# Two-block network on one core: the local-attention chain of each head pair is spread over more of the next pair's projections

## What is computed

```python
def second_block(x, ...):
    for l in range(DEPTH):                      # 2 layers
        h = rms_norm_2(x, mix_norm_g[l])
        proj = h @ w_in[l]
        sb_q, sb_k, sb_v, sw_q, sw_k, sw_v, gate_logits = jnp.split(proj, split_at, axis=-1)
        o_sb = stick_breaking_attention(sb_q, sb_k, sb_v)
        q = apply_rope(rms_norm_2(sw_q, q_norm_g[l]), cos, sin)
        k = apply_rope(rms_norm_2(sw_k, k_norm_g[l]), cos, sin)
        y_swa = sliding_window_sink_attention(q, k, sw_v, sinks[l]) @ w_branch_swa[l]
        ...
        x = x + merged @ w_out[l]
        x = x + jnp.square(jax.nn.relu(rms_norm_2(x, mlp_norm_g[l]) @ w_up[l])) @ w_down[l]

def sliding_window_sink_attention(q, k, v, sinks):
    # a block of 128 queries sees its own block of keys and the one before it
    scores = jnp.einsum('bnqkgd,bnskd->bnkgqs', qb, k_band) * scale
    scores = jnp.where(valid, scores, -jnp.inf)
    probs = jax.nn.softmax(jnp.concatenate([scores, sink], axis=-1), axis=-1)[..., :-1]
    return jnp.einsum('bnkgqs,bnskd->bnqkgd', probs, v_band)
```

## Time and profile before

| | us |
|---|---|
| runs | 2957.77, 2960.5, 2960.77 |
| profiled execution | 2960.41 |
| its span, first to last instruction | 2958.6 |
| TensorE busy | 2815.6 (95%) |
| VectorE busy | 1515.0 (51%) |
| ScalarE busy | 1167.7 (39%) |
| GpSimd busy | 89.5 (3%) |

### The profile page before, as it was taken

One profiled execution on the slowest core, in us unless ns is written; L12 is line 12 of the kernel. 1 busy time (PEld: TensorE's weight loads), 2 busy tenths in 40 slices (PEclk: granted clock), 3 DMA queues, 4 the chain that ended last, 5 costly groups with the idle time before them and its releaser, 6 DMA issues.

```text
span 2958.6 us, 30829 instructions
## 1 busy us (share of the span) xinstructions
PE 2815.6 (95%) x12462; PEld 2219.0 (75%) x12462; DVE 1515.0 (51%) x2101; ACT 1167.7 (39%) x1736; POOL 89.5 (3%) x64
## 2 busy tenths in 40 slices
PE   7799889999998999998999999999989999999998
PEld 6677777888877888886555788888865657888887
DVE  3555557564767666577334445343543434544343
ACT  4443325343456433244444434222434444333222
POOL 1321210000000000000000000000000000000000
PEclk9899999999998999999999999999999999999999
DMA  3111112222322322222111122222221112222322
GB/s 142 54 54 54 43 41 78 100 94 99 106 87 79 112 100 93 100 96 89 36 36 43 57 93 100 99 94 100 94 71 36 41 38 71 93 96 97 100 96 75
DMA packets 66813, 235.66 MB, mean 80 GB/s; under 512 B 7408, under 2 KB 8176, under 8 KB 66672
## 3 DMA queue, kind: packets, MB, share of 16 engines
q1 hardware_dynamic: 62064, 226.00, 22.3%
q10 hardware_dynamic: 4608, 7.70, 0.7%
HBM read 231.57 MB, written 2.10 MB: 79 GB/s over the span
## 4 chain that ended last, share of the span: by engine, by line
PE 87%; DVE 7%; ACT 4%; issue 1%; POOL 0%; ACTq 0%; DVEq 0%
PE bank L392 25%; PE bank L394 25%; PE bank L393 25%; ACT w_hi_k L839 1%; PE bank L700 1%; PE bank L711 1%; PE bank L749 1%; DVE w_lo_k L1290 1%; PE bank L691 1%; PE bank L703 1%; PE bank L760 1%; PE bank L767 1%; DVE xr_lru L1577 1%; PE bank L527 0%; DVE land_r_mix L1413 0%
## 5 line engine op out<-in xcount | busy, mean ns | idle before, releaser
L392 PE MATMUL bank<-x_hi_k,w_hi_k 128*128 128x512 f32 x2152 | 883.2, 410 | 22.9 <-DVE x_lo_k L1297 18.5
L839 ACT ACTIVATE w_hi_k<-raw_k 128x1024 fp32r<-128x1024 f32 x431 | 454.6, 1058 | 1012.5 <-PE bank L394 1012.4
L394 PE MATMUL bank<-x_hi_k,w_lo_k 128*128 128x512 f32 x2152 | 849.6, 395 | 0.0
L393 PE MATMUL bank<-x_lo_k,w_hi_k 128*128 128x512 f32 x2152 | 848.4, 394 | 0.0
L1290 DVE TENSOR_TENSOR w_lo_k<-raw_k,w_hi_k 128x1024 fp32r<-128x1024 f32 x431 | 528.8, 1227 | 182.4 <-ACT w_hi_k L839 182.3
L392 PEld LDWEIGHTS bank<-x_hi_k,w_hi_k 128*128 128x128 f32 x2152 | 412.2, 192 | 115.2 <-DVE x_lo_k L1297 20.5
L393 PEld LDWEIGHTS bank<-x_lo_k,w_hi_k 128*128 128x128 f32 x2152 | 411.7, 191 | 86.9 <-issue 5.7
L394 PEld LDWEIGHTS bank<-x_hi_k,w_lo_k 128*128 128x128 f32 x2152 | 410.1, 191 | 88.7
L392 PE MATMUL bank<-y_hi_k,w_hi_k 128*128 128x512 f32 x1136 | 448.2, 395 | 15.5 <-DVE w_lo_k L1290 7.6
L394 PE MATMUL bank<-y_hi_k,w_lo_k 128*128 128x512 f32 x1136 | 444.6, 391 | 0.0
L393 PE MATMUL bank<-y_lo_k,w_hi_k 128*128 128x512 f32 x1136 | 444.4, 391 | 0.0
(11 more groups left out here) (319 smaller groups left out, 2562.1 us busy)
## 6 DMA issues: line engine op xcount, KB each, us to landing
raw_k<-wstream SPq DMA_DIRECT2D x431, 512.0 KB, 3.2
h_k<-xT ACTq DMA_DIRECT2D x8, 256.0 KB, 7.7
outT<-h_k ACTq DMA_DIRECT2D x8, 256.0 KB, 3.3
decay_mix<-constants ACTq DMA_DIRECT2D x4, 256.0 KB, 2.7
levels_mix<-constants ACTq DMA_DIRECT2D x1, 448.0 KB, 8.8
vec_k<-vectors ACTq DMA_DIRECT2D x1, 286.5 KB, 4.6
cos_mix<-constants ACTq DMA_DIRECT2D x1, 256.0 KB, 8.3
sin_mix<-constants ACTq DMA_DIRECT2D x1, 256.0 KB, 8.4
```

Source lines behind the costliest of these rows:

```text
L392: pe.matmul(dst, wh, rh, start=start, stop=False)
L393: pe.matmul(dst, wh, rl, start=False, stop=False)
L394: return pe.matmul(dst, wl, rh, start=False, stop=stop)
L839: act.activation(k.w_hi[:, u % SPLIT, :], k.raw[:, u % RAW, :], ACT.Copy).then_inc(*hi_done.mark())
```

## The change

The local part gets 21 steps where it had 17, by empty ones, and ends at place 0.85 where it ended at 0.8. No instruction is added, removed or altered. A step of the local part is 0.85/21 = 0.0405 of a pair where it was 0.8/17 = 0.0471. TensorE's sum stands one step later and its scores of half 0 two steps later than the count would have had them, and each half has one more empty step between scores and transposes. ScalarE and VectorE get empty steps ahead of the exponentials, the rotation, the maxima and behind the exponentials and scalings. The places, as shares of a pair:

| | sum | scores 0 | transposes 0 | scores 1 | transposes 1 | output 1 |
|---|---|---|---|---|---|---|
| TensorE before | 0.047 | 0.235 | 0.424 | 0.518 | 0.706 | 0.753 |
| TensorE after | 0.081 | 0.283 | 0.486 | 0.567 | 0.769 | 0.810 |

| | scaled query | rotation | maxima 0 | scaling 0 | maxima 1 | scaling 1 |
|---|---|---|---|---|---|---|
| VectorE before | 0.094 | 0.141 | 0.282 | 0.376 | 0.565 | 0.659 |
| VectorE after | 0.121 | 0.162 | 0.324 | 0.405 | 0.607 | 0.688 |

ScalarE's exponentials move from 0.329 and 0.612 to 0.364 and 0.648.

```diff
-WINDOW_STEPS = 2 + 2 + 2 * 6 + 1
+WINDOW_STEPS = 6 + 2 * 7 + 1
...
-    return ((stick, STICK_STEPS, 0, 1), (window, WINDOW_STEPS, 0, 0.8),
+    return ((stick, STICK_STEPS, 0, 1), (window, WINDOW_STEPS, 0, 0.85),
...
     def window(layer, m):                      # TensorE
         at = (layer, m)
+        yield
         pe.wait_ge(*act_done.at("wq_sq", *at))
         pe.matmul(bank[6][:], k.halves, k.sq, start=True, stop=True).then_inc(*mark("wq_sum", *at))
+        yield
         yield
...
             mm.then_inc(*mark("scores", *at, half))
+            yield
             yield
...
+        yield                                  # ScalarE, behind the inverse root
+        yield
...
                            bias=vcol("sinks2", layer * 8 + m + half * 4)).then_inc(*mark("exps", *at, half))
+            yield
             yield
...
     def window(layer, m):                      # VectorE
         at = (layer, m)
         yield
+        yield
         dve.wait_ge(*act_done.at("wq_root", *at))
...
         rope(k.wq, k.rot).then_inc(*mark("wq", *at))
+        yield
         yield
...
                                   ALU.mult).then_inc(*mark("probs", *at, half))
+            yield
             yield
```

## The result

The changed kernel takes 2920.16 us (median of 4 runs, 2918.82 to 2920.77), against 2959.14 us for the kernel before (4 runs). The ratio is 0.9868, with a 95% interval from 0.9852 to 0.9883. Its profiled execution took 2920.77 us, 39.6 us less than the 2960.41 of before. The forecast had been 2932, with a range from 2921 to 2947, so the sign and the mechanism held.

The account below looks back on a forecast made before the run. TensorE, busy 95%, was taken as the bound, so only its idle time and clock could pay: 2960.4 - 14.4 (waits) - 21.3 (low clock) + 7.1 (low stretches kept) = 2931.8, 2932 us, range 2921 to 2947.

Parts of the forecast that it names:

- The start: Start of a pair: value transposes moved into the sum's wait gain only 0.08 us; wait splits into about 1.2 and 0.45.
- The scores: Scores of half 0: the wait for the rotated query falls to 0 to 0.1 us; gain so far 1.90 us.
- The transposes: L760: half 0 waits 0.9 us instead of 0.53, taking back 0.4; half 1 about 1.25 instead of 1.48.
- What a pair gives: Whole attention pair at full clock: 1.90 - 0.4 + 0.3 = 1.8 us shorter, 14.4 us in all.
- The corner: Best case of the range: no low stretch and 0.4 us a pair more, both L760 waits at 0.7; 2921.5 us.
- The clock: Attention pairs: most of 21.3 us lost to low clock returns; two pairs of eight keep 3.55 each, together 7.1.
- The low stretches stay: Rival, attention pairs: low-clock stretches come in the same number behind other gaps; 2946.0 us, chance 0.20.
- slower: Rival: clock falls in every pair, from the scores to the next logits, at 5.38 us each; 2967.7 us, chance 0.04.
- The waits only change places: Rival: rotation and probabilities come 0.8 us later each, 1.8 us a pair shrink to 0.2; 2959 us, chance 0.06.

Follow-up runs that it names:

- shifted kernels: Two kernels: the changed kernel with the matmul of the key's sum of squares made once and twice more ahead of each layer's pairs; 2920.31 and 2922.0 us.

## Why the prediction was wrong, and where it was right

The step that failed is the sum for a pair at full clock: 1.8 us were said and 2.65 measured. The paths behind it were the right ones.

**The start: right.** L691 was worked out to start 1.41 us behind the sum and does. The two waits came out as 1.29 and 0.29 us, where 1.2 and 0.45 had been said.

**The scores: right in kind.** Their wait is gone from the list, where 0 to 0.1 us was expected. They start 8.72 us behind the sum, where 1547.02 - 1538.12 = 8.90 had been worked out.

**The transposes: right in kind, sized 0.2 too long each.** The new neighbours do hold them. Predicted were waits of 0.9 and 1.25 us, measured 0.70 and 1.06. For half 0 the terms of the chain from the last scores to the transposes sum to 11.3 us, and it took 1417.87 - 1407.01 = 10.86, so 0.4 us of its links overlap where 0.1 to 0.2 had been allowed.

**What a pair gives: the term that failed.** The sum said 1.8 us, the trace says 2.65. The listed waits of the third pair were 5.56 us before, and those of a pair are 3.34 now, 2.22 less, where the working had them at 3.8, 1.8 less. The other 0.43 us aren't waits. TensorE's own spacing shrank where narrow matmuls came to stand side by side: from the last scores to what follows is 1407.01 - 1406.47 = 0.54 us, where before it was 1550.27 - 1549.64 = 0.63. The logits of 384 columns take 1407.74 - 1407.01 = 0.73, before 1552.92 - 1552.08 = 0.84. The two starts of before that the earlier trace rows leave out are, in TensorE's timeline of its third pair:

```profile
1549.64 0.70 PE L749 MATMUL bank<-wk_att,wq_att 64*128 64x256 f32 x2
...
1552.92 0.23 PE L692 MATMUL bank<-mask_b_att,id_b_att 128*128 128x128 bf16 x1
```

These two make 0.20 of the 0.43; the rest is spread over many places of the pair, and part of it can be how idle time is counted, from modelled ends. The prediction costed a matmul the same wherever it stands. Over eight pairs this term is 6.8 of the 11 us missed. The range allowed 0.4 us a pair for it, and 0.85 were needed. The corner was miscounted too: with both L760 waits at 0.7, as it says, a pair gives (0.9 - 0.7) + (1.25 - 0.7) = 0.75 us more, and the range would have begun near 2919, below what was measured. The term would have been as wrong. That these shorter spacings come from the neighbours is read from the two traces; no run isolates it.

**The clock: right in mechanism, better than assumed.** The low stretches followed the idle time ahead of the scores, as said: behind the scores they were gone without that wait and back with most of it, as the table above counts. I kept two pairs at the mean price of before, 7.1 us. It was three at 1.4, 4.2 us, behind the start and not behind the scores. That is 2.9 us of the miss, and the shifted kernels show that the number is chance between none and three. The last 1.4 us lie outside the pairs, where no step of the change reaches. 0.4 of them lie ahead of the first pair. The other 1.0 lies between the two layers' pairs. There TensorE idles for 3.75 us in both kernels, and the clock falls around the end of it, for 6.8 us before and for 3.4 after. This is the piece of before:

```profile
2154.80:2161.50 6.70, 5.50 (x11) 3.71 (x12) 1.14 (x2) 2.37 (x3) 0.00 (x0) 0.50 0.24 78
```

In the two shifted kernels, where the work is that of the changed one, the same place is low for 3.4 and for 6.8 us. So this hangs on the start as well and is no part of the change.

**The rivals.** "The low stretches stay" and "slower" fell with the clock of the pairs. The first was right in one point: the three that are left come behind the start, whose idle time now lies in two pieces. None begins behind the idle time and the eight transposes of L763, in 16 places. "The waits only change places" is true in part: of 41.6 us, 26.7 are still waits.

## What to carry to other kernels

Of a shift of many steps, find the one instruction whose wait costs most and move that alone: here a single step on one engine gave the whole gain, and the other moves put softplus instructions ahead of the chain that TensorE needed next. A short wait on TensorE can cost more than its length, since the clock may fall behind it, so stretches of equal work are worth laying side by side with their granted clock. Before moving cheap work into a wait, look for the second operand that comes just behind the first: it takes the wait over.

## What the runs showed of the hardware

An idle time of 1.3 to 1.8 us on TensorE can be followed by a stretch at 1.2 GHz, in some places and not in others. Behind the 1.73 us at the start of a pair it never followed, in 42 pairs of six kernels. Behind 1.29 us with four transposes ahead of it, it followed in three pairs of eight, and in one and none of the same eight pairs in two kernels in which they started at other times. Ahead of the scores it followed 1.4 to 1.8 us of idle time in 11 pairs of 13 and 0.2 us in 6 of 32, and never came there without a listed wait, in 43 pairs. The granted clock of a stretch of narrow matmuls can't be told from its idle time alone.
